# Four high products, then their four low ones, in a two-layer encoder's projections

## The reference

```
for l in range(DEPTH):                       # DEPTH = 2
    h = rmsnorm(x, norm_mix[l])
    proj = h @ w_in[l]                       # 2048 x 6144: q, k, v, gate_b, gate_c, u
    ...                                      # rotary on q, k; differential attention, 8 heads
    o_conv = short_gated_conv(gate_b, gate_c, u, conv_w[l])
    x = x + concatenate([o_attn, o_conv]) @ w_out[l]        # 2048 x 2048
    h = rmsnorm(x, norm_ffn[l])
    x = x + (silu(h @ w_gate[l]) * (h @ w_up[l])) @ w_down[l]   # 2048 x 5632 twice, 5632 x 2048
return rmsnorm(x, norm_final)
```

## Time and profile before

| | us |
|---|---|
| median of 3 runs | 2268.09 |
| lowest, highest | 2266.25, 2269.67 |
| the profiled execution | 2267.71 |
| its span, first to last instruction | 2265.9 |

### The profile page before, as it was taken

The page is one execution under the profiler, slowest core; times in us unless marked ns, Lnnn a source line. Parts: engine busy times, 40 slices in busy tenths (PEclk is TensorE's granted clock), DMA queues, the critical chain, the costliest instruction groups (busy, mean ns, idle before and its releaser), DMA issues.

```text
span 2265.9 us, 29670 instructions
## 1 busy us (share of the span) xinstructions
PE 2241.1 (99%) x12040; PEld 1917.3 (85%) x12040; DVE 1354.1 (60%) x1837; ACT 1083.2 (48%) x1623; POOL 137.7 (6%) x186
## 2 busy tenths in 40 slices
PE   9999999999999999999999999999999999999998
PEld 7888878888888888888888888788888888888886
DVE  5666675566665656444456676756656565654443
ACT  5445555545454545444444555545545454544443
POOL 0131120000000000000001323100000000000000
PEclk9999999999999999999999999999999999999999
DMA  7654545565655565555566545556565655556552
GB/s 262 214 186 163 172 148 189 184 196 176 205 176 196 186 195 185 191 192 197 192 192 207 183 155 175 169 176 198 175 197 186 193 187 197 186 187 215 193 191 106
DMA packets 308937, 423.34 MB, mean 187 GB/s; under 512 B 13504, under 2 KB 196416, under 8 KB 308672
## 3 DMA queue, kind: packets, MB, share of 16 engines
q1 hardware_dynamic: 305968, 414.30, 55.6%
q0 software_dynamic: 1536, 4.20, 0.7%
q10 hardware_dynamic: 1296, 2.94, 0.4%
HBM read 415.10 MB, written 2.10 MB: 184 GB/s over the span
## 4 chain that ended last, share of the span: by engine, by line
PE 96%; POOL 1%; ACT 1%; DVE 1%; issue 0%; DMA 0%; ACTq 0%
PE bank L1037 41%; PE bank L1040 21%; PE bank L1063 11%; PE bank L1064 11%; PE bank L1065 11%; POOL ev L379 1%; PE bank L1112 1%; PE bank L1135 0%; ACT whi L427 0%; PE bank L1091 0%; DVE wlo L655 0%; PE bank L1121 0%; PE bank L1074 0%; POOL o_ms L370 0%; DMA sin_r<-tables_dram 0%
## 5 line engine op out<-in xcount | busy, mean ns | idle before, releaser
L655 DVE TENSOR_TENSOR wlo<-raw,whi 128x1024 fp32r<-128x1024 f32 x784 | 957.4, 1229 | 580.8 <-ACT whi L427 579.9
L1037 PE MATMUL bank<-xg,whi 128*128 128x512 f32 x4096 | 1294.0, 397 | 5.9 <-DVE wlo L655 5.8
L427 ACT ACTIVATE whi<-raw 128x1024 fp32r<-128x1024 f32 x784 | 818.3, 1059 | 707.7 <-PE bank L1040 411.9
L1040 PEld LDWEIGHTS bank<-xg,wlo 128*128 128x128 f32 x4096 | 770.6, 188 | 182.3
L1040 PE MATMUL bank<-xg,wlo 128*128 128x256 f32 x4096 | 806.3, 278 | 0.0
L1037 PEld LDWEIGHTS bank<-xg,whi 128*128 128x128 f32 x4096 | 625.1, 189 | 8.8 <-issue 6.7
L1063 PE MATMUL bank<-whi,hidden 128*128 128x512 f32 x704 | 274.8, 390 | 2.6 <-DVE wlo L655 2.6
L1064 PE MATMUL bank<-wlo,hidden 128*128 128x512 f32 x704 | 274.6, 390 | 0.0
L1065 PE MATMUL bank<-whi,hidden 128*128 128x512 f32 x704 | 274.6, 390 | 0.0
L435 ACT ACTIVATE ev<-bank 128x256 f32<-128x256 f32 x256 | 84.4, 381 | 240.0 <-PE bank L1040 240.0
L662 DVE TENSOR_TENSOR ev<-bank,ev 128x256 f32<-128x256 f32 x224 | 84.7, 420 | 161.0 <-ACT ev L435 161.0
(11 more groups left out here) (103 smaller groups left out, 1043.7 us busy)
## 6 DMA issues: line engine op xcount, KB each, us to landing
raw<-w_in_dram SPq DMA_DIRECT2D x192, 512.0 KB, 4.8
raw<-w_gate_dram SPq DMA_DIRECT2D x176, 512.0 KB, 3.6
raw<-w_up_dram SPq DMA_DIRECT2D x176, 512.0 KB, 4.7
raw<-w_down_dram SPq DMA_DIRECT2D x176, 512.0 KB, 4.5
raw<-w_out_dram SPq DMA_DIRECT2D x64, 512.0 KB, 4.6
swapped<-qk POOLq DMA_DIRECT2D x32, 128.0 KB, 2.8
resid<-x_dram SPq DMA_DIRECT2D x8, 256.0 KB, 8.3
final_gain<-gain_dram ACTq DMA_DIRECT2D x1, 1024.0 KB, 6.1
```

Source lines behind the costliest of these rows:

```text
L427: act.activation(whi[:, blk.slot(k)], raw[:, slot, half * UNIT_KT:(half + 1) * UNIT_KT, :], ACT.Copy).then_inc(hi_ready, 1)
L655: dve.tensor_tensor(wlo[:, blk.slot(k)], raw[:, slot, half * UNIT_KT:(half + 1) * UNIT_KT, :], lo_bits(whi[:, blk.slot(k)]), ALU.subtract) ...
L1037: pe.matmul(b[j][:], whi[:, blk.slot(k), i, w[j]], moving[:, kt, :], start=(kt == 0), stop=False, skip_group_check=True)
L1040: done = pe.matmul(b[j][:, 0:S], wlo[:, blk.slot(k), i, w[j]], moving[:, kt, 0:S], start=False, stop=final, skip_group_check=True)
```

## The change

`products` goes over the tiles in another grouping. In a call of one unit it still takes tiles in pairs; in a call of two units it takes one tile at a time. In both cases there are four combinations of tile and contraction tile: the four high matmuls of all of them come first, then the four low ones. `tile_free` waits for the last tile of the group that begins, so for one bank at a time in calls of two units. `unit_taken` is raised behind the last low matmul of a unit, as before. Below it in the file, every line number is higher by two; the low matmul is L1042 in the new one.

```diff
-                for pair in range(0, BT, 2):
-                    js = (pair, pair + 1)
+                together = 1 if len(ks) > 1 else 2
+                for first in range(0, BT, together):
+                    js = range(first, first + together)
                     b = {j: bank[blk.bank(j)] for j in js}
                     w = {j: slice(P * cols[j], P * (cols[j] + 1)) for j in js}
                     if ks[0] == 0:
-                        tile_free(blk, pair + 1)
-                    for k in ks:
-                        for i in range(UNIT_KT):
-                            kt = UNIT_KT * k + i
-                            final = k == blk.units - 1 and i == UNIT_KT - 1
-                            for j in js:
-                                pe.matmul(b[j][:], whi[:, blk.slot(k), i, w[j]], moving[:, kt, :], start=(kt == 0),
-                                          stop=False, skip_group_check=True)
-                            for j in js:
-                                done = pe.matmul(b[j][:, 0:S], wlo[:, blk.slot(k), i, w[j]], moving[:, kt, 0:S],
-                                                 start=False, stop=final, skip_group_check=True)
-                                if final:
-                                    done.then_inc(tile_done, 1)
-                        if pair == BT - 2 and k < blk.units - 1:
+                        tile_free(blk, js[-1])
+
+                    kts = [(k, i, UNIT_KT * k + i) for k in ks for i in range(UNIT_KT)]
+                    for k, i, kt in kts:
+                        for j in js:
+                            pe.matmul(b[j][:], whi[:, blk.slot(k), i, w[j]], moving[:, kt, :], start=(kt == 0),
+                                      stop=False, skip_group_check=True)
+                    for k, i, kt in kts:
+                        final = kt == UNIT_KT * blk.units - 1
+                        for j in js:
+                            done = pe.matmul(b[j][:, 0:S], wlo[:, blk.slot(k), i, w[j]], moving[:, kt, 0:S],
+                                             start=False, stop=final, skip_group_check=True)
+                            if final:
+                                done.then_inc(tile_done, 1)
+                        if js[-1] == BT - 1 and i == UNIT_KT - 1 and k < blk.units - 1:
                             done.then_inc(unit_taken, 1)
```

## The result

The changed kernel takes 2274.69 us (median of 9 runs, 2272.44 to 2276.35). The kernel before took 2268.03 us in 9 runs beside them (2266.02 to 2270.07). The ratio is 1.0031, with a 95% interval from 1.0022 to 1.004: 6.7 us more, where 2.6 us less was forecast. The time lies inside the forecast's range, but that range (2254.5 to 2277) held gains and losses alike, so this says little. The sign is that of one of the rivals, the debt of the lows, which had given 2279.5.

What follows compares the result with a forecast made beforehand. TensorE, busy 99% of the span, was taken as the bound. Four highs at 925 ns and four lows at 465 made 1390 instead of 1392.5 ns; over 1024 groups, 2.6 us off 2267.71 gave 2265.1 us, range 2254.5 to 2277.

Steps and rivals of the forecast that it cites:

- the debt of the lows: Rival, slower: third and fourth low take 120 ns each, highs behind stay slow; 11.8 us more, 2279.5 us; chance 0.16.
- What bounds the kernel, and where to read it: TensorE, busy 99% of the span, sets the time; read matmul starts and counts in a stretch, not durations.
- The own pace of the highs: 512-column matmuls in a stream of their own follow each other every 226.4 ns.
- Four highs, 925 ns: Four high matmuls in a row behind lows take 925 ns, 19 ns over four of their own pace.
- Four lows, 465 ns: Four low matmuls behind highs: 230 ns for the first two, 235 for the third and fourth.
- How I chose between the bounds: Per group, bounds of 1364 and 1420 ns; 1390 taken near the middle, from matmuls of the same width.
- Banks, bank waits: One bank per group in two-unit calls, and PE's waits for free banks: gain and cost put at nothing.
- Late release: Two-unit calls free the earlier weight slot 1.16 us later; about 0.9 us delay against 3.9 us of slack.
- The fixed toll: Rival, faster: each turn between highs and lows costs a fixed amount, now halved; 2259 or 2254 us; chance 0.35.
- No change at all: Rival: each matmul following a low pays for its load in either order; 1392.5 ns stay, 2267.7 us; chance 0.17.

## Why the prediction was wrong

- **What bounds the kernel, and where to read it**: right. PE's closeness is all that moved, and no wait was added.
- **The own pace of the highs** (226.4 ns): right; in runs of eight the last three come back to 227.
- **Four highs, 925 ns**: nearly right, 929. They are 3 ns cheaper than before, where the sum had some 5 (two times 465 less 925).
- **Four lows, 465 ns**: this is the step that failed. From the starts they take 474: 117.5 and 119.6, then 118.8 and 118.3. Most of the miss is in the first two, 237 ns where the sum had 230. These were taken from the earlier trace rows, where a run of two lows stands behind two highs at their own pace, and runs of two lows cost 230 to 233 in every order seen. That the first two of a run of four would cost the same was taken over without a reason, and it doesn't hold in the changed kernel; it does hold behind eight highs, so why not behind four stays open. The third and fourth, 235 in the sum, measured 237. They were taken from scores that work in pairs on half of the rows, and of the two rows I took the cheaper. The misses, 4 + 7 + 2 ns, turn 2.5 ns won into 10 lost.
- **How I chose between the bounds**: the term of the lows was read from places with another history than the one it was used for. The sum was 2.5 ns out of 1392, from rows read to 10 ns; it could not carry a sign, and 0.39 for faster was too much on it.
- **Banks, bank waits**: right, shown by the runs with single and with alternating banks. **Late release**: right in kind, a little low in size. In a gate/up block that begins at 1707.79, unit 4's conversion starts at 1713.44, 5.65 us in, where it was 4.46 us in before: 1.2 us later, not 0.9. In both kernels it starts some 0.3 us behind the point where PE passes the release, a distance that the prediction had taken for slack. Its subtraction starts at 1714.54, 0.7 us later in the block than before. PE waits no longer for it:

```profile
1707.79 0.40 PE L1037 MATMUL bank<-xg,whi 128*128 128x512 f32 x1
...
1713.44 1.06 ACT L427 ACTIVATE whi<-raw 128x1024 fp32r<-128x1024 f32 x1 [1.41 <-PE bank L1042]
...
1714.54 1.23 DVE L655 TENSOR_TENSOR wlo<-raw,whi 128x1024 fp32r<-128x1024 f32 x1 [0.81 <-ACT whi L427]
```

- **The debt rival** gave the right sign and nearly the size: 1404 per eight against 1402.3. Its total of 11.8 us was too high mainly because it counted all 1024 groups; the convolution's gate blocks paid 0.14 us in six. That it met the size is partly luck: its split, 232 for the first two lows and 240 for the others, was 237 and 237. Its picture, that longer runs only add debt, is wrong as a rule: runs of eight are better than of four, and runs of one the worst.
- **The fixed toll** is half right. There is a toll for each turn, as runs of one show, but it isn't fixed: one run of highs and one of lows together cost 6 ns over own pace in runs of one, 3 in runs of two, 16 in runs of four and 18 in runs of eight.
- **No change at all** is ruled out, as the interval of the ratio leaves out 1. The loads behind lows of 256 columns start on time, and the cost hangs on the order. The Trainium skill ("TensorE: Matmul & The Clock Gate", Back-to-back issue gap) has each warm matmul at N / 2.4 + 2.5 ns. For the fp32r matmuls of one length the trace has 13.3 ns in place of 2.5; for the bf16 ones of 512 columns at the start it agrees, 216 ns (eight from 6.61 to 8.34 us).

What stays open is which part of TensorE makes the toll, and why it is 3 ns per two highs and two lows with 256 columns, 8 with 288, 26 with 384 and nothing with 512. (With 192 columns it is some 39, 679 less an estimated own pace of 640, but there the loads are late as well.) No other order that was run is faster than the kernel before. The order of highs and lows has at most 1392.5 - 1387 = 5.5 ns per eight left to win, some 5 us over 1024 eights, if mixing cost nothing.

## What to carry to other kernels

In this kernel, where TensorE is the bound and matmuls of two lengths mix, the order was worth 0.3 to 0.65% with nothing else changed, and it doesn't get better or worse steadily with the length of the runs: one, two, four and eight gave 1412, 1392, 1402 and 1396 ns. Price a new order from starts in a place with the same neighbours in front, and not only with the same matmul; where there is none, run it rather than argue it. A sum whose result is smaller than the grain of the rows that it is built from carries no sign.

## What the runs showed of the hardware

Matmuls of one length follow each other at their columns at 2.4 GHz and 13.3 ns: 226.7 ns for 512 columns, 120 for 256, in fp32r. Where lengths meet, up to five of the 512-column ones behind a run of 256-column ones take 228 to 236 ns. The pace hangs on the order of lengths and not on the banks (the same mean durations, 395 and 278 ns, and 2298 and 2299 matmuls in 400 us, with one bank or two). Cutting a 256-column matmul to 192 saved 36 us where its columns at 2.4 GHz are worth 109; the second low of a pair didn't shrink, and the weight load behind it came 23 or 24 ns late.
